# Seven taps of a depthwise convolution as TensorE products with diagonal matrices

## The reference, cut to what matters

```
def _conformer_conv(h, i, p, seg_len):
    z = h @ p['w_pw1'][i] + p['b_pw1'][i]          # 1024 -> 2048
    z = z[..., :D] * jax.nn.sigmoid(z[..., D:])    # GLU
    zr = z.reshape(n * segs, seg_len, D)
    zr = conv_depthwise(zr, p['conv_k'][i])        # width 31, zero padded, one filter per channel
         + p['conv_b'][i]
    z = _layernorm(zr, p['lnc_g'][i], p['lnc_b'][i])
    return jax.nn.silu(z) @ p['w_pw2'][i] + p['b_pw2'][i]
```

## Time and profile before

| | |
|---|---|
| median of three executions | 3414.64 us |
| the profiled execution | 3413.74 us |
| its span, first to last instruction | 3411.9 us |
| mean granted TensorE clock over the span | 0.971 |
| busy share PE / DVE / ACT / POOL | 95% / 64% / 32% / 13% |
| share of PE in the chain of work that ended last | 88% |
| the convolution stage: first `pw1` product to first `pw2` product | 1887.69 us to 2088.17 us |

### The profile page before, as it was taken

One profiled execution on the slowest core, in us unless ns is written; L12 is line 12 of the kernel. 1 busy time (PEld: TensorE's weight loads), 2 busy tenths in 40 slices (PEclk: granted clock), 3 DMA queues, 4 the chain that ended last, 5 costly groups with the idle time before them and its releaser, 6 DMA issues.

```text
span 3411.9 us, 64317 instructions
## 1 busy us (share of the span) xinstructions
PE 3228.1 (95%) x23962; PEld 2689.3 (79%) x23962; DVE 2182.6 (64%) x4215; ACT 1091.7 (32%) x1625; POOL 444.3 (13%) x194
## 2 busy tenths in 40 slices
PE   8898898899999999999999768899999999999998
PEld 2684875799998888888877424899998888887876
DVE  0455364596766777767853893696767777667843
ACT  0332231333233333333233432433323333332333
POOL 0430000455000000000000460554000000000000
PEclk9897999999999999999999888999999999999999
DMA  8342011334333333333333223333333333333331
GB/s 299 130 142 99 4 52 29 105 118 124 108 101 123 117 117 122 115 120 111 105 117 98 62 86 99 100 124 121 108 105 120 115 121 117 117 123 105 110 118 68
DMA packets 103839, 373.19 MB, mean 109 GB/s; under 512 B 12320, under 2 KB 14368, under 8 KB 103456
## 3 DMA queue, kind: packets, MB, share of 16 engines
q1 hardware_dynamic: 103712, 371.40, 34.5%
HBM read 369.52 MB, written 1.84 MB: 109 GB/s over the span
## 4 chain that ended last, share of the span: by engine, by line
PE 88%; DVE 6%; issue 3%; ACT 1%; DMA 1%; POOL 0%; DVEq 0%; ACTq 0%; SPq 0%
PE bank L1200 35%; PE bank L1282 32%; PE bank L961 4%; PE bank L1148 3%; PE bank L990 3%; PE bank L1259 2%; PE bank L943 2%; PE bank L1274 1%; DVE arena L1804 1%; PE bank L934 1%; DMA ring<-in_w_tiles 1%; PE bank L1210 1%; DVE arena L1812 0%; PE bank L971 0%; DVE gated L1389 0%
## 5 line engine op out<-in xcount | busy, mean ns | idle before, releaser
L1200 PE MATMUL bank<-h_parts,split 128*128 128x384 f32 x6912 | 1268.8, 339 | 21.9 <-POOL h_parts L586 19.9
L1200 PEld LDWEIGHTS bank<-h_parts,split 128*128 128x128 f32 x6912 | 1197.2, 189 | 29.3 <-issue 17.3
L1282 PE MATMUL bank<-split,coef_parts 128*128 128x512 f32 x4608 | 1105.2, 395 | 10.3 <-DVE coef_parts L1731 10.2
L646 ACT ACTIVATE split<-ring 128x1024 fp32r<-128x1024 f32 x544 | 575.7, 1059 | 1367.4 <-PE bank L1282 695.8
L1282 PEld LDWEIGHTS bank<-split,coef_parts 128*128 128x128 f32 x4608 | 855.1, 189 | 184.3 <-DVE coef_parts L1731 10.7
L1724 DVE TENSOR_TENSOR split<-ring,split 128x1024 fp32r<-128x1024 f32 x440 | 536.3, 1219 | 142.8 <-ACT split L646 142.5
L579 POOL TENSOR_TENSOR split<-ring,split 128x1024 fp32r<-128x1024 f32 x104 | 263.5, 2537 | 656.2 <-ACT split L646 656.2
L1731 DVE TENSOR_TENSOR coef_parts<-gated,coef_parts 128x384 fp32r<-128x384 f32 x256 | 141.9, 555 | 279.5 <-ACT coef_parts L824 279.3
L1701 DVE TENSOR_TENSOR hot_i<-iota_h,routes_t 128x1536 f16<-128x1536 f16 x256 | 243.4, 951 | 10.7 <-ACT gated L799 10.7
L961 PE MATMUL bank<-ring,silc 128*2 128x512 f32 x384 | 175.7, 616 | 17.3 <-DMA ring<-in_w_tiles 10.4
L1772 DVE SCALAR_TENSOR_TENSOR gated<-bank,gated 128x384 f32 (+1 forms) x128 | 71.3, 557 | 142.1 <-PE bank L1259 142.1
(11 more groups left out here) (244 smaller groups left out, 2623.0 us busy)
## 6 DMA issues: line engine op xcount, KB each, us to landing
ring<-in_e_u SPq DMA_DIRECT2D x256, 512.0 KB, 3.6
ring<-in_e_v SPq DMA_DIRECT2D x256, 512.0 KB, 3.5
ring<-in_w_tiles SPq DMA_DIRECT2D x183, 512.0 KB, 4.2
x_sb<-in_x_t SPq DMA_DIRECT2D x2, 768.0 KB, 7.3
y_t<-gated SPq DMA_DIRECT2D x4, 384.0 KB, 2.5
smallm<-in_mixer SPq DMA_DIRECT2D x1, 1375.5 KB, 8.9
smallm<-in_mixer SPq DMA_DIRECT2D x1, 1375.0 KB, 8.6
small<-in_small SPq DMA_DIRECT2D x1, 736.0 KB, 4.4
```

The costliest lines, as they stand in the source:

```text
L646: act.activation(split[:, 2 * p_ * D:(2 * p_ + 1) * D], ring[:, r * D:(r + 1) * D], ACT.Copy)\
L1200: mm = pe.matmul(out, part(e, x, c * P, (c + 1) * P), hp4[:, y, c, :], start=(c == 0 and x == 0 and y == 0), stop=(c == DC - 1 and x == 1))
L1282: mm = pe.matmul(bank[2 * b + hf][:, :], cp4[:, sl, x, b * P:(b + 1) * P], part(e, y, hf * 512, (hf + 1) * 512), start=False, stop=True, s ...
```

## The change

DVE's share of the taps becomes 24 (0 to 23) and the other seven (24 to 30) go to PE. For each chunk ACT makes seven 128x128 diagonal matrices: the identity times the tap's per-channel weight. PE multiplies each with the shifted chunk `zc`, accumulating in bank 6 or 7, and `conv_join` adds that bank in place of POOL's sum. POOL's tree and ACT's 12 tap products are gone. On PE, `mod_rows(10)` moves into the last turn of the loop, and `mod_rows(11)` moves from behind the variance to ahead of the last chunk's taps.

```diff
-DVE_TAPS = 19
-POOL_TAPS = CONV_W - DVE_TAPS
-TAP_STEP, TAP_ROUND = 4, 4
+DVE_TAPS = 24
+PE_TAPS = CONV_W - DVE_TAPS
+TAP_ROUND = 4
...
-        prod = ar(CO + 9216 + 7 * T, 2 * POOL_TAPS * T).rearrange("p (s w t) -> p s w t", s=2, t=T)
+        diag = ar(CO + 9216 + 7 * T, DC * PE_TAPS * P).rearrange("p (m w c) -> p m w c", m=DC, c=P)
...
-            for m in range(DC):
-
-                pool.wait_ge(prod_ready, POOL_TAPS * (m + 1))
-                pr = prod[:, m % 2]
-                q = POOL_TAPS // 4
-                pool.tensor_tensor(pr[:, 0:2 * q], pr[:, 0:2 * q], pr[:, 2 * q:4 * q], ALU.add).then_inc(pool_tap, 1)
...
-                if m >= 2:
-                    act.wait_ge(pool_tap, 4 * m - 4)
-                with act.Fori(0, POOL_TAPS // TAP_STEP) as it:
...
+                for w in range(PE_TAPS):
+                    k = DC * (DVE_TAPS + w) + m
+                    act.activation(diag[:, m, w, :], sm("ident"), ACT.Copy, scale=sm("conv_k", k, k + 1))\
+                       .then_inc(diag_ready, 1)
             mod_evac(10)
+            mod_evac(11)
...
-            mod_evac(11)
...
+            def taps(m):
+
+                pe.wait_ge(halo_done, 2 * m + 2)
+                pe.wait_ge(diag_ready, PE_TAPS * (m + 1))
+                if m >= 2:
+                    pe.wait_ge(conv_done, m - 1)
+                for w in range(PE_TAPS):
+                    t = DVE_TAPS + w
+                    mm = pe.matmul(bank[6 + m % 2][:, 0:T].rearrange("p (r t) -> p r t", t=ROW), diag[:, m, w, :],
+                                   zc[:, m, :, t:t + ROW], start=(w == 0), stop=(w == PE_TAPS - 1))
+                mm.then_inc(tap_mm, 1)
+
             pe.wait_ge(out_used, 16)
...
+                if m == 7:
+                    pe.wait_ge(glu_done, 7)
+                    mod_rows(10)
+                if m >= 1:
+                    taps(m - 1)
                 if m >= 3:
                     mean(m - 3)
-            pe.wait_ge(glu_done, 7)
-            mod_rows(10)
+            pe.wait_ge(glu_done, 8)
+            mod_rows(11)
+            taps(DC - 1)
...
             mod_turn(10)
-            mod_rows(11)
-            pe.wait_ge(conv_act, 8)
             mod_turn(11)
...
-                linear(POS["pw2"] + m, bank[m % 4][:, 0:T], hs)
+                linear(POS["pw2"] + m, bank[m % 4][:, 0:T], hs, conv_act if m == 0 else None)
...
-                dve.wait_ge(pool_tap, 4 * (m + 1))
+                dve.wait_ge(tap_mm, m + 1)
                 dve.wait_ge(conv_tap, DVE_TAPS * (m + 1))
                 st.link(dve.tensor_tensor(acc[:, m, :], acc[:, m, :], accs[:, m, :], ALU.add))
-                dve.tensor_tensor(acc[:, m, :], acc[:, m, :], acq[:, m, :], ALU.add).then_inc(conv_done, 1)
+                dve.tensor_tensor(acc[:, m, :], acc[:, m, :], bank[6 + m % 2][:, 0:T], ALU.add)\
+                   .then_inc(conv_done, 1)
...
                 conv(m, 0, 2)
-                with dve.Fori(0, (DVE_TAPS - 3) // TAP_ROUND) as it:
+                conv(m, 0, 3)
+                with dve.Fori(0, (DVE_TAPS - 4) // TAP_ROUND) as it:
                     for t in range(TAP_ROUND):
-                        conv(m, it, 3 + t)
+                        conv(m, it, 4 + t)
```

More of the change, by code:

```diff
@@ L345, in build_trunk @@
         conv_tap = sem("conv_taps_added")
-        prod_ready = sem("conv_products_ready")
-        pool_tap = sem("conv_products_added")
+        diag_ready = sem("conv_diagonals_ready")
+        tap_mm = sem("conv_tap_products")
         conv_done = sem("conv_chunks_done")
```

## The result

The changed kernel takes 3389.29 us (median of four, 3386.85 to 3390.41) against 3414.53 us of the kernel before (median of four): ratio 0.9924, 95% interval 0.9907 to 0.9941. The forecast was 3387 in 3379 to 3402. The profiled execution took 3386.85 us, its span is 3385.0 us.

What follows compares the result with a forecast made beforehand. DVE, slowed by POOL's adds, was taken to set the stage's end, and PE's own work after the change. 19.4 us at the last mean plus 8.3 in the tail made 27.7 us: 3387 us, range 3379 to 3402.

Steps and rivals of the forecast that it cites:

- DVE is held up by POOL's adds, not by ACT: Convolution on DVE: chunk 1 took 26.98 us beside POOL's adds, undisturbed chunk 0 took 10.73 with ACT's products running.
- Undisturbed chunks of 13.40 and 13.97 us: DVE's time per chunk without POOL's adds and with five more multiply-adds: 13.40 us without a join, 13.97 with one.
- A tap product costs what a dense one costs, 0.645 us: PE's 56 tap products: gapped reads cost nothing more than dense ones, 0.645 us each, 36.1 us in all.
- Rivals 1: PE's tap products cost 0.80 us each, 8.7 us more, 3396 us; chance 0.22 together with tile waits of that size.
- rival 2: PE reads the gapped operand at half pace, 1.29 us a product, 36.1 us more, 3423 us, slower; chance 0.05.
- PE sets the last mean by its own sum: PE works without waiting from pw1 to the last mean: 153.7 us, ending at 2041.4, 19.4 us earlier.
- A loop turn of 15.5 us: PE's loop turn, 10.31 + 4.5 + 0.645 = 15.5 us, exceeds DVE's 13.97, so DVE is early in each.
- The tail: Last mean to pw2, with pw2's low-clock loss: 19.0 us against 27.34, 8.3 us gained despite a new wait for mod_add(10).
- Rival 3: The clock does not fall in the tail, since the turns count as work: 3383 us; chance 0.15.
- Sum: Whole gain: 19.4 us at the last mean plus 8.3 in the tail, 27.7 us.
- Rival 4: DVE stays slow, with chunks of 27 us as before, and only the tail gains: 3427 us; chance 0.02.
- The pairs of end times: DVE instructions ending with POOL's adds, 1917.00 and 1916.78, 1955.47 and 1955.05: taken to agree with the shared-port rule.

Runs made afterwards that it cites:

- e3: Kernel before without POOL's 32 adds, eleven of ACT's twelve products per chunk left out of the sum (layer not computed): 3346.94 us, ratio 0.9801 to the kernel before.
- e5: Changed kernel with POOL's 32 adds put back, on zeros that nobody reads: 3431.44 us, ratio 1.0045 to the kernel before.
- e6: Kernel of e2 with 25 taps on DVE and six on PE: 3382.55 us, ratio 0.9900 to the kernel before.
- e7: Kernel of e2 with 26 taps on DVE and five on PE: 3378.81 us, ratio 0.9891 to the kernel before.
- e2: Changed kernel with mod_rows(11) put back behind the variance, between mod_turn(10) and mod_turn(11): 3380.69 us, ratio 0.9899 to the kernel before.
- e4: Changed kernel with mod_turn(10) ahead of the last chunk's taps and mod_add(10) between the last two joins: 3386.68 us, ratio 0.9919 to the kernel before.

## Why the prediction was right

- *DVE is held up by POOL's adds, not by ACT.* Right, shown from both sides: taking the adds away saves 69 us (e3), putting them back costs 45 (e5).
- *Undisturbed chunks of 13.40 and 13.97 us.* Measured 13.37 (1899.24 to 1912.61) for the first and 13.95 (1925.98 to 1939.93) for chunk 2; the 22 multiply-adds took 11.72, where 22 x 0.534 is 11.75.
- *A tap product costs what a dense one costs, 0.645 us.* Measured 0.650. Rivals 1 (0.80) and 2 (1.29) fell. The rule of the Trainium skill (SBUF — State Buffer, "Door 1: The DMA port swizzle") on 16-byte lines, by which I reckoned 2.3 us more, hardly shows here: 56 x 0.005 is 0.3 us. (The prediction gives the section before that one as its place.)
- *PE sets the last mean by its own sum.* Right: 153.7 us forecast, 154.7 measured from the first product. e6 shows that PE's products count one for one (5.2 of its 5.7 us), e7 where that ends.
- *A loop turn of 15.5 us.* 1954.75 to 1970.27, 15.52.
- *ACT's diagonals and the moved rows hide or run at full pace.* No PE wait for either; `mod_rows` 13.89 us, so no late tile.
- *The tail: a new wait for mod_add(10), low clock behind it.* Right in kind, 1.5 us too good in size: the pause is 5.50 us, `mod_turn(11)` 3.54 in place of 3.0, and `pw2` loses 44.53 - 41.55 = 3.0 in place of 2.3. The 3.0 came from a turn during which the granted clock was 0.60 on average (106.08 to 109.08 us in the trace before), not 0.50; the 2.3 from a first chunk at whose start the clock stayed low for 4 us (1887.69 to about 1892). Here `pw2` began at 2058.07 and the clock rose about 2064, 6 us later. Rival 3 fell.
- *Sum.* 27.7 us forecast, 25.3 measured in the stage: 1.0 short in PE's sum and 1.4 in the tail. Of the 1.0, half is the taps (0.3 for 0.650 in place of 0.645, 0.2 at the two sets that follow `mod_rows`) and half the means, mainly the last three, which take 2.31 us in place of 1.94. The two errors have the same sign, so nothing cancels in the stage. That the profiled execution (3386.85) came within 0.9 us of my 3386.0 is luck: its stage started 1.8 us earlier.
- *Rival 4, DVE stays slow,* did not occur. e5 shows about what it would have been: 3431 us, against the 3427 that I gave it. Its "chunks of 27 us as before" holds for every second chunk only; the sum did not use it. Its chance and that of rival 2 make 0.07 for slower, where I wrote 0.06.
- *The pairs of end times.* The first pair (1917.00 and 1916.78) is a `tensor_scalar` with one tensor input, which the rule as the prediction gives it, for two inputs, does not cover; the trace shows that it waited too, 4.24 us in place of 0.48. The single multiply-add of 5.40 us (under e3) has two inputs and is the better evidence.

What the prediction did not say, and e2 shows: of its two parts, taps and reorder, the reorder works against the result. I credited the tail with 8.3 us and did not set against it the 13.8 us that `mod_rows(11)` adds to PE's sum ahead of the mean. The sum was right, since it held both, but a reader could have taken the move for a gain; it costs 8.3 us.

## What to carry to other kernels

Ask first which engine's instructions are stretched, and compare their ends with those of the neighbour's: a helper engine that adds up products for DVE can cost DVE more than doing the work itself (an estimate, not run: twelve taps at 0.534 us are 51 us for eight chunks, and POOL's adds for them cost the stage 69 us in e3). Once the bound has moved to another engine, reckon every moved piece anew by that engine's sum: work put into its idle time is free, work put ahead of a serial tail is not, and the best place for independent work is the pause inside the tail. And a pause of 5.50 us on PE cost more than itself here: the 3.0 us longer `pw2` and the 1.6 us longer turn behind it ran at the low clock.

## What the runs showed that I had not expected

A PE pause of 2.88 us (e4) already made `pw2` 1.7 us longer, and in e6 the clock fell to 0.50 (2056 to 2058) with no pause over 1.2 us in the 20 us ahead of it, only `mod_rows` between two turns of two-column products and a 1.15 us wait; in e2 and e7, with the same order of work there, it stayed at 1.00. Which of these pieces lets it fall was not settled.
